# Expert queries projected with the query weights as the stationary operand

## The reference

```python
def peer(x, w_query, sub_keys, expert_u, expert_v):
    ...
        q = (xb @ w_query).reshape(PEER_BLOCK, PEER_HEADS, 2, half)
        s1 = jnp.einsum('thd,kd->thk', q[:, :, 0], sub_keys[0], ...)
        s2 = jnp.einsum('thd,kd->thk', q[:, :, 1], sub_keys[1], ...)
        v1, i1 = lax.top_k(s1, PEER_TOPK)
        v2, i2 = lax.top_k(s2, PEER_TOPK)
        ...
        act = jnp.einsum('td,thkd->thk', xb, expert_u[eidx], ...)
        coef = (gate * jax.nn.gelu(act)).astype(xb.dtype)
        return jnp.einsum('thk,thkd->td', coef, expert_v[eidx])
```

## Time and profile before

| | |
|---|---|
| three runs, median | 4244.62 us (4236.45 to 4249.43) |
| profiled execution | 4237.36 us, its span 4235.6 us |
| busy share: PE, VectorE, ScalarE, GpSimd | 78%, 70%, 15%, 59% |
| moved by the gathers (queue q0) | 1165.57 MB of 1405.11 MB |
| first gather | 779.41 us after the span's start |

### The profile page before, as it was taken

How to read it: one execution, slowest core, us unless ns; L and a number is a source line. 1 busy time by engine, 2 the same in 40 slices (tenths; PEclk the granted TensorE clock), 3 DMA queues, 4 the chain that set the end, 5 groups by cost and what they waited for, 6 DMA issues and landing times. The chain is left out here.

```text
span 4235.6 us, 33993 instructions
## 1 busy us (share of the span) xinstructions
PE 3297.4 (78%) x9798; PEld 1765.9 (42%) x9798; DVE 2973.6 (70%) x6507; ACT 641.5 (15%) x1759; POOL 2484.7 (59%) x2277
## 2 busy tenths in 40 slices
PE   6978897788888987787888888887777665565666
PEld 1445575654444543464444444444444222222222
DVE  2212211688886788988878887887887788878885
ACT  0020001211012211122100132111111111101010
POOL 0001000577765576566777665776677777777776
PEclk9969898899987898898989788998889888888888
DMA  7316344799997899999999888999999999999998
GB/s 254 122 42 169 99 127 148 294 406 404 392 351 274 313 390 388 346 392 375 395 401 389 344 319 284 390 389 387 382 406 373 389 407 386 404 406 402 390 398 342
DMA packets 578894, 1405.11 MB, mean 332 GB/s; under 512 B 44731, under 2 KB 276347, under 8 KB 578683
## 3 DMA queue, kind: packets, MB, share of 16 engines
q0 software_dynamic: 320080, 1165.57, 71.2%
q1 hardware_dynamic: 223070, 196.45, 14.9%
q10 hardware_dynamic: 35560, 40.91, 2.7%
HBM read 1369.31 MB, written 33.44 MB: 331 GB/s over the span
## 5 line engine op out<-in xcount | busy, mean ns | idle before, releaser
L1787 PE MATMUL peer_psA<-peer_vring,peer_diag 128*128 128x512 f32 x2464 | 1396.5, 707 | 622.2 <-DMA peer_vring<-in_expert_v,peer_idx 504.2
L1501 POOL DMA_INDIRECT peer_uring<-in_expert_u,peer_idx x1088 | 1224.3, 1125 | 762.7 <-DVE peer_idx L2406 318.3
L1511 POOL DMA_INDIRECT peer_vring<-in_expert_v,peer_idx x1088 | 1218.5, 1120 | 551.0 <-issue 316.6
L2431 DVE CUSTOM_DVE_ANT_0 peer_uring<-peer_uring,peer_h 128x1024 f32<-128x1024 f32 x768 | 923.0, 1222 | 224.5 <-DMA peer_uring<-in_expert_u,peer_idx 222.0
L1787 PEld LDWEIGHTS peer_psA<-peer_vring,peer_diag 128*128 128x128 f32 x2464 | 510.6, 221 | 1350.1 <-issue 1191.0
L2447 DVE SCALAR_TENSOR_TENSOR peer_acc<-peer_vring,peer_coef,peer_acc 128x1024 f32<-128x1024 f32 x463 | 595.0, 1285 | 65.4 <-DMA peer_vring<-in_expert_v,peer_idx 61.5
L2431 DVE CUSTOM_DVE_ANT_0 peer_uring<-peer_uring,peer_psB 128x1024 f32<-128x1024 f32 x320 | 382.2, 1218 | 128.2 <-DMA peer_uring<-in_expert_u,peer_idx 127.9
L1756 PE MATMUL peer_psB<-peer_w,keep_hT 128*128 128x256 f32 x1152 | 274.2, 394 | 22.2 <-DMA peer_w<-in_w_query 21.1
L1682 PE MATMUL peer_psB<-keep_hT,peer_w 128*128 128x384 f32 (+1 forms) x864 | 276.4, 479 | 2.5 <-DMA peer_w<-in_w_in 2.5
L1756 PEld LDWEIGHTS peer_psB<-peer_w,keep_hT 128*128 128x128 f32 x1152 | 228.6, 200 | 79.4 <-issue 26.9
L1700 PE MATMUL peer_psB<-keep_hT,peer_w 128*128 128x384 f32 (+1 forms) x768 | 248.3, 478 | 6.4 <-DMA peer_w<-in_w_attn_o 6.4
(11 more groups left out here) (245 smaller groups left out, 3023.8 us busy)
## 6 DMA issues: line engine op xcount, KB each, us to landing
peer_w<-in_w_in SPq DMA_DIRECT2D x102, 512.0 KB, 18.0
peer_w<-in_w_query SPq DMA_DIRECT2D x24, 1024.0 KB, 15.5
peer_w<-in_w_in SPq DMA_DIRECT2D x12, 1536.0 KB, 18.2
peer_uring<-in_expert_u,peer_idx POOLq DMA_INDIRECT x1088, 8.3
peer_vring<-in_expert_v,peer_idx POOLq DMA_INDIRECT x1088, 8.2
front_ring<-in_w_ada POOLq DMA_DIRECT2D x7, 2048.0 KB, 8.4
front_ring<-in_w_ada SPq DMA_DIRECT2D x5, 2048.0 KB, 8.1
peer_w<-in_w_conv_o SPq DMA_DIRECT2D x24, 384.0 KB, 14.4
```

The costliest lines, as they stand in the source:

```text
L1501: pool.indirect_dma_start(out=uring[:, r % U, :], out_offset=None, in_=io["expert_u"], in_offset=bass.IndirectOffsetOnAxis(ap=idx[:, s % 4 ...
L1511: pool.indirect_dma_start(out=vring[:, r % V, :], out_offset=None, in_=io["expert_v"], in_offset=bass.IndirectOffsetOnAxis(ap=idx[:, s % 4 ...
L1787: last = pe.matmul(psA[:, c * 512:(c + 1) * 512], diag[:, a % DG, :], vring[:, r % V, c * 512:(c + 1) * 512], start=first, stop=False, ski ...
L2431: dve.tensor_tensor_reduce(uring[:, r % U, :], uring[:, r % U, :], rows, 1.0, 0.0, ALU.mult, ALU.add, act_[:, k:k + 1]).then_inc(u_used, 1)
```

## The change

The roles of the operands are exchanged: the query weights are stationary and the turned rows of all three tiles (384 columns) move. A head is then two products of 8 matmuls, one for each half, and its result is already turned; `project` and `turn_q` with their copies go, and two copies of 384 columns a head take their place. The order becomes: the turning of the segment's last tile, then for each head its two products and, one head behind, the three scores of the head before. The turned queries have four slots of one head each, in the room of `mT`.

```diff
@@ chain_order
-        first, n = g * SEG * HEADS, SEG * HEADS
-        for i in range(n + 2):
-            if i == 2:
-                order += [("turn", g, SEG - 1, c) for c in range(2)]
-            order += [(name, first + i - lag) for lag, name in enumerate(("project", "turn_q", "score"))
-                      if 0 <= i - lag < n]
+        order += [("turn", g, SEG - 1, c) for c in range(2)]
+        for h in range(HEADS + 1):
+            if h < HEADS:
+                order += [("query", g, h, c) for c in range(2)]
+            if h:
+                order += [("score", (g * HEADS + h - 1) * SEG + i) for i in range(SEG)]
@@ chain_cost, last_chain_of
-    return {"project": 3.4, "qkv": 5.1, "s": 1.2, "o": 1.5, "t": 0.6}.get(name, 0.5)
+    return {"query": 5.1, "qkv": 5.1, "s": 1.2, "o": 1.5, "t": 0.6}.get(name, 0.5)
...
-    return "project", (g * HEADS + j) * SEG + SEG - 1
+    return "query", g, j, 1
@@ peer
-        qn, qT, sc_out = n.sb("qn", [P, 2, K2]), n.sb("qT", [P, 2, K2]), n.sb("sc_out", [P, 2, K2])
+        sc_out = n.sb("sc_out", [P, 2, K2])
+        QS = 4
+        qT = flat[:, 0:QS * 2 * M].rearrange("p (s c m) -> p s c m", s=QS, c=2)
+        sub_rows = flat[:, 0:K2]
@@ queries (TensorE)
+                yield from turn(g, SEG - 1)
+                for h in range(HEADS + 1):
+                    if h < HEADS:
                         wv = slot(("wq", g, h))[:, 0:DC * KD].rearrange("p (c m) -> p c m", c=DC)
...
+                            ready(("wq", g, h))
+                            for i in range(SEG):
+                                wait_emptied(pe, ("turn", g, i, 1))
+                            dst = opened(key)
+                            for k in range(DC):
+                                last = pe.matmul(dst[:, 0:M], wv[:, k, c * P:(c + 1) * P], hT[:, k, :],
+                                                 start=(k == 0), stop=(k == DC - 1))
...
+                    for i in range(SEG if h else 0):
+                        key = ("score", (g * HEADS + h - 1) * SEG + i)
...
+                            last = pe.matmul(dst[:, c * KEYS:(c + 1) * KEYS],
+                                             qT[:, (h - 1) % QS, c, i * P:(i + 1) * P], skT[:, c, :],
+                                             start=True, stop=True)
@@ keep_queries (ScalarE)
+                yield from keep_turned(g, SEG - 1)
+                for h in range(HEADS + 1):
+                    for c in range(2 if h < HEADS else 0):
+                        key = ("query", g, h, c)
+                        yield number[key]
                         wait_filled(act, key)
...
+                        if h >= QS:
+                            wait_filled(act, ("score", (g * HEADS + h - QS) * SEG + SEG - 1))
+                        act.activation(qT[:, h % QS, c, :], bank(key)[:, 0:M], ACT.Copy).then_inc(out_of(key), 1)
...
+                    if g + 1 < SEGS_N and h in (2, 4, 6):
+                        yield from norm_root(g + 1, h // 2 - 1)
@@ norm_root, norm_shift
-                yield number["score", (g - 1) * SEG * HEADS + 5 + 5 * i]
+                yield number["score", (g - 1) * SEG * HEADS + 5 + 6 * i]
@@ shift_tile (VectorE)
-                yield number["out", g, i + 1, 0] if i + 1 < SEG else number["project", g * SEG * HEADS]
+                yield number["out", g, i + 1, 0] if i + 1 < SEG else number["turn", g, SEG - 1, 0]
```

72 lines of the change are left out of this document (14 added, 58 removed).

## The result

The changed kernel takes 4320.5 us (median of 4 runs, 4313.0 to 4329.4) beside 4240.5 us for the kernel before (4 runs, 4227.7 to 4249.4): a ratio of 1.0187, 95% interval 1.0166 to 1.0207, so about 79 us slower. The forecast was 4254 us, with a range of 4234 to 4274. The profiled executions took 4237.4 (before) and 4329.4 us.

A forecast was written before the change was run, and what follows sets the result against it. Expert gathers were taken to bound the stretch from 780 to 1240 us, the lead delaying all behind it. Terms 9.7 - 4.6 + 1 + 3 = +9.1 us, on the three-run median 4244.6, gave 4254 us, range 4234 to 4274.

The forecast's parts named there:

- the last assumption: Attention in segments 1 and 2: its dips in transfer rate would not change by more than 10 us.
- The moved steps of the normalisation: Two later steps of segment 1's first normalisation move by an item or two under the same gathers: 0 us.
- The burst rival: Three scores at once into two slots make ScalarE wait for stores: +11 to +22 us, 4265 to 4276; chance 0.20.
- ScalarE's room: Argument against the burst: ScalarE waits 54.9 us in 6 times for VectorE's gate input, and the stall fits there.
- the 380 named as a sign of being wrong: Query stretches with three scores a head: below 380 GB/s the forecast would be wrong.
- The lead: Before the first gather: tile turning, four heads and seven scores take 50.9 us against 41.2, +9.7 us; bounds +7 and +13.
- cheap wide products: Rival in query products: 384 columns cost no more than 256, 226 ns; lead -3.3, sum -3.9, 4241 us; chance 0.04.
- the slow start: In the lead, the first 32 projection instructions took 10.14 us against 7.24 after them; 2.9 us stays.
- the 4.6 us given back: Query blocks 6 and 7 and a tile of x load before the gathers, freeing gather time: -4.6 us; ends 0 and 6.6.
- The query starts: Where queries begin: segment 1 +1 us (ends -4, +5), segment 2 +3 us (ends 0, +12) from a later weighing.
- Off the path at 0: Under the gathers: 28.1 us of query transposes and four of nine ScalarE copies a head go, costed at 0.

The follow-up runs named there:

- The swap: Query prices alone exchange the places of hidden work: changed kernel with the old places 4275.3 us, kernel before with the changed kernel's places 4290.5 us.
- the new pace: Changed kernel at its own places of hidden work, with six score buffers instead of two: 4298.6 us, ratio to before 1.0141.
- after_old_pace: Changed kernel with two query prices in its cost table, so all other chains run where they ran before: 4275.3 us, ratio to before 1.0094.
- the woven order and six buffers: Changed kernel ordered half 0, previous head's score 0, half 1, scores 1 and 2; places of before, six score buffers: 4242.2 us, 1.0008.
- the best one: Attention prices raised by half and TensorE's chunks to (i+2)/n: 4180.3 us in the woven six-buffer kernel with old places, 4183.1 us in the kernel before.
- old_pace_six: Changed kernel with the places of before, by two query prices, and six score buffers instead of two: 4266.0 us, ratio to before 1.0066.
- dearer attention and a shorter chunk: Kernel before with attention's three prices raised by half and TensorE's chunks to (i+2)/n instead of (i+3)/n: 4183.1 us, ratio 0.9865.

## Why the prediction was wrong, by its own steps

- **The step that failed** is the last assumption: that attention's dips do not change by more than 10 us "because they meet as many weighed rows as before". They changed by 14.2 and 12.6 us. Behind it, the sum had no term at all for where the hidden work runs, though prices and marks had changed. The swap prices this at 39 us in one kernel and 54 in the other, of the 79, and by the windows attention has 23 and 26 us of it; the rest lies mostly where queries start and end. The moved steps of the normalisation were put at 0 in the same way; no run prices them alone.
- **The burst rival** was right in its mechanism and in its size, but was not alone: ScalarE's waits came to 120.2 us, five times, and cost 20 us at the new pace (12 at the old), inside the 11 to 22 that it was given. ScalarE's room, 54.9 us of waits for VectorE (counted from 1760 us; from 1780 it is 50.9 in 5), was no cover at the end of segment 1's queries, where the DMA share fell from 0.98 to 0.83 and the gathers to 308 GB/s, under the 380 named as a sign of being wrong.
- **The lead**: +9.7 forecast, +8.8 measured. A wide instruction takes 10.49/32 = 328 ns, the convolution's 327.5; cheap wide products are refuted. The four heads took 22.74 + 2 x 10.49 = 43.7 us, for 44.8 with the slow start. Blocks 6 and 7 were issued ahead of the gathers as foreseen; the 4.6 us given back can't be seen by themselves.
- **The query starts**: +1 and +3 forecast, 10.7 and 15.8 measured. With the places of before they are 4.7 and 5.4 us (after_old_pace, 341 GB/s over 160 us and 373 over 200, beside 353 and 384), and with the woven order and six buffers 2.8 and 3.5 (346 and 377). In the changed kernel GpSimd waited there 19.5 us at most at segment 1 (14 forecast) and 23.8 at segment 2 (28 forecast, from 10.91 us to which the profile gives no releaser), but at segment 1 a second wait of 16.3 us came with it, as TensorE waited for VectorE's shifted rows three times, 35.5 us, for 21.5 in two before.
- **Off the path at 0** held as far as the runs tell: with the woven order and six buffers beside it, the loss of the transposes gave nothing, at the old pace (1.0008) and at the best one (4180 and 4183 us).

So most of the terms that were worked out stand within a few us where the places stay as they were, and the missing term was some five times their sum of 9.1 us. Even at the old places and with six buffers the changed order stands 28 us above the kernel before (old_pace_six). The lead has 8.8 of them; the 16 that the woven order takes away, apart from the lead, had no term either.

## What to carry to other kernels

Where a table of costs sets the place of hidden work, a change of one entry, or of the key that a mark names, moves all the rest: first compare at equal places, by giving the new kernel the old places and the old kernel the new ones. Work that leaves an engine in bunches wants buffers for the bunch, or an order that parts it (here six buffers ended the waits of a bunch of three; three were not tried). Read the waits of a ring of buffers for all engines that free it together. And price a chain by what it takes in the trace, waits included: dearer attention and a shorter chunk were worth 57 us here, the change of the queries nothing that could be measured.

## What was not expected of the hardware

Stores of 128 KB under full gathers held ScalarE up to 8.9 us, though their median time to land was 6.6 us before, and in attention of segment 1 TensorE was busy 199 of 240 us before and 190 after, at granted clocks of 0.78 and 0.77, while 289 and 265 GB/s moved beside it: a busy share of 83 and 79% did not show that the gathers waited.
